# Second block of a two-block transformer kernel: ten gate tiles moved beside the mixers, the merge as a phase of its own, output projection by token halves with the last norm

## The reference, cut to what matters

```python
h = _rms_norm(x, g_pre)
proj = h @ w_in + b_in            # 54 column tiles of 128 for the mixers, then 40 for the gates
# five mixers, each 512 wide: y_a (gated delta rule), y_b (31-tap convolution, layer norm),
# y_c (sliding window with sinks), y_d (linear recurrence), y_e (cross attention); y_x = mixer * silu(z_x)
branch_out = jnp.einsum('bsnw,nwd->bsnd', ys, w_br)
gate = jax.nn.sigmoid(gates.reshape(B, S, N_BRANCHES, D_MODEL))
merged = jnp.sum(gate * branch_out, axis=2)
y = merged @ w_out
x = x + _rms_norm(y, g_post)      # mean over the 1024 columns of one token
```

## Time and profile before

| | us |
|---|---|
| median of 3 runs | 3455.55 (3450.47 to 3455.75) |
| the profiled execution's own time | 3458.23 |
| its span in the trace | 3456.4 |
| TensorE busy in the span | 3206.3 (93%) |
| first to last `gemm` unit of the second block, and the rest up to the end | 1602.0 to 3411.2, 45.2 |

### The profile page before, as it was taken

One profiled execution on the slowest core, in us unless ns is written; L12 is line 12 of the kernel. 1 busy time (PEld: TensorE's weight loads), 2 busy tenths in 40 slices (PEclk: granted clock), 3 DMA queues, 4 the chain that ended last, 5 costly groups with the idle time before them and its releaser, 6 DMA issues. The chain is left out here.

```text
span 3456.4 us, 36380 instructions
## 1 busy us (share of the span) xinstructions
PE 3206.3 (93%) x14817; PEld 2466.1 (71%) x14817; DVE 1443.4 (42%) x1849; ACT 1097.4 (32%) x1632; POOL 669.2 (19%) x317
## 2 busy tenths in 40 slices
PE   6999988879999999995999999999999999999995
PEld 4765544447788888874767787777777888888874
DVE  3113333536414141475456877668552213223123
ACT  4334433323312030342453322223434323223122
POOL 2222111014222222242121000011111222222220
PEclk9999999889999999997999999999999999999997
DMA  3211000013111111123332121104334221221121
GB/s 125 97 63 60 19 0 1 1 64 108 49 49 46 48 48 49 49 89 137 100 108 92 37 68 44 61 34 141 110 110 164 92 98 49 98 98 49 49 92 55
DMA packets 105933, 246.19 MB, mean 71 GB/s; under 512 B 8232, under 2 KB 49448, under 8 KB 105640
## 3 DMA queue, kind: packets, MB, share of 16 engines
q1 hardware_dynamic: 97992, 215.56, 19.3%
q10 hardware_dynamic: 7776, 28.32, 2.0%
HBM read 187.74 MB, written 55.05 MB: 70 GB/s over the span
## 5 line engine op out<-in xcount | busy, mean ns | idle before, releaser
L1676 PE MATMUL psum<-normed_hi,w_hi 128*128 128x512 f32 x1632 | 674.3, 413 | 42.4 <-POOL w_lo L2218 35.2
L1678 PE MATMUL psum<-normed_hi,w_lo 128*128 128x512 f32 x1632 | 639.4, 392 | 0.0
L1677 PE MATMUL psum<-normed_lo,w_hi 128*128 128x512 f32 x1632 | 638.2, 391 | 0.0
L2218 POOL TENSOR_TENSOR w_lo<-buffer,w_hi 128x1024 fp32r<-128x1024 f32 x122 | 310.0, 2541 | 1500.8 <-ACT w_hi L1250 1500.8
L1676 PEld LDWEIGHTS psum<-normed_hi,w_hi 128*128 128x128 f32 x1632 | 308.8, 189 | 114.9 <-POOL w_lo L2218 36.7
L1678 PEld LDWEIGHTS psum<-normed_hi,w_lo 128*128 128x128 f32 x1632 | 307.6, 188 | 66.1
L1677 PEld LDWEIGHTS psum<-normed_lo,w_hi 128*128 128x128 f32 x1632 | 308.9, 189 | 63.7 <-issue 8.0
L2839 POOL TENSOR_TENSOR w_lo<-buffer,w_hi 128x1024 fp32r<-128x1024 f32 x88 | 212.4, 2415 | 724.9 <-ACT w_hi L2757 724.9
L1250 ACT ACTIVATE buffer<-psum,par 128x512 f32<-128x512 f32 (+1 forms) x196 | 138.0, 705 | 518.6 <-PE psum L1678 503.4
L2719 PE MATMUL psum<-hidden_hi,w_hi 128*128 128x512 f32 x512 | 200.9, 392 | 3.1 <-POOL w_lo L2839 3.1
L2719 PE MATMUL psum<-normed_hi,w_hi 128*128 128x512 f32 x512 | 200.1, 391 | 3.3 <-POOL normed_lo L2846 2.2
(11 more groups left out here) (393 smaller groups left out, 5438.5 us busy)
## 6 DMA issues: line engine op xcount, KB each, us to landing
buffer<-in_w_mlp SPq DMA_DIRECT2D x72, 512.0 KB, 3.6
buffer<-in_w_in SPq DMA_DIRECT2D x70, 512.0 KB, 4.9
scratch_in<-buffer ACTq DMA_DIRECT2D x54, 512.0 KB, 2.9
buffer<-in_w_gate SPq DMA_DIRECT2D x40, 512.0 KB, 3.6
buffer<-scratch_in SPq DMA_DIRECT2D x32, 512.0 KB, 6.5
buffer<-scratch_y SPq DMA_DIRECT2D x20, 512.0 KB, 7.7
buffer<-in_w_br SPq DMA_DIRECT2D x20, 512.0 KB, 3.6
buffer<-in_w_o SPq DMA_DIRECT2D x16, 512.0 KB, 3.7
```

The costliest lines, as they stand in the source:

```text
L1676: pe.matmul(out, hi, xh, start=k == 0, stop=False)
L1677: pe.matmul(out, hi, xl, start=False, stop=False)
L1678: mm = pe.matmul(out, lo, xh, start=False, stop=k == unit.kc - 1)
L2218: pool.tensor_tensor(ws.lo[:, n % 2], raw[:, n % 2], ws.hi[:, n % 2].bitcast(F32), ALU.subtract).then_inc(w_lo, 1)
```

## The change

The second block becomes two phases. (1) `mixer_phase` keeps only the mixers and the input projection, and ten of the forty gate tiles (tiles 6 and 7 of each branch, `EARLY_GATES`) are put among the input tiles: `Stream` has 130 units where the part up to the end of the input projection had 110. The planned end stays at 1040 (`T_END`, once `T_MERGE`), so that units 34 to 86 are planned in the 466 us that held 34 to 74, and 86 to 130 in the 324 us that held 74 to 110. The early gates are evicted with the sigmoid and stored to HBM. (2) `merge_phase` has the other 30 gate tiles, the branches and the output projection, with a ring of six PSUM banks; the stored gates come back by SP for the last two tiles of each branch. (3) The output projection runs all eight tiles for the first 512 tokens and then all eight for the last 512, so each of its weight tiles is loaded and split twice (16 slots where there were 8); each half is squared, summed, scaled, added to the residual (3 of 8 tiles by GpSimd) and stored in 256 KB pieces, the first half beside the second half's matmuls. The last norm phase is gone. In the first block `raw` and `w_hi`, `w_lo` only get their names elsewhere, at the same addresses.

```diff
+EARLY_GATES = [b * DC + t for b in BRANCHES for t in (DC - 2, DC - 1)]
+IN2_ORDER = (list(range(12, 16)) + list(range(12))
+             + ["ab", 16, 17, 28, 29, 54, 18, 19, 24, 25, 55, 26, 27, 20, 21, 56, 30, 31, 32, 57, 33, 22, 23, 58]
+             + [34, 35, 36, 37, 59, 38, 39, 40, 41, 60, 42, 43, 44, 45, 61, 46, 47, 48, 49, 62, 50, 51, 52, 53, 63])
...
-    pace = Pace((0, 0.0), (34, 250.0), (74, T_AFTER), (110, T_MERGE), (st.n_merge, T_MERGE + 654.0),
-                (st.n_merge + 16, T_MERGE + 742.0))
+    pace = Pace((0, 0.0), (34, 250.0), (86, T_AFTER), (len(st.units), T_END))
...
-                            run(halves(res[:, q % 3])[h], ps, ACT.Identity, bias=shift).then_inc(kept_act, 1)
+                            run(halves(res[:, q % 3])[h], ps, ACT.Identity if j < N_IN2 else ACT.Sigmoid, bias=shift).then_inc(kept_act, 1)
...
+            def ends():
+                yield T_END + 60.0
+                for r in range(3):
+                    sp.wait_ge(stored[r], 16 * ((len(held) + 2 - r) // 3))
+                for r in range(2):
+                    sp.wait_ge(wy_out[r], 8 * U)
+                sp.wait_ge(conf_out, 16 * BT)
+                sp.wait_ge(o_out, 16 * NB)
+                sp.wait_ge(lru_out, 16 * BT)
...
+                self.slots.append(("br", tiles[0]))
+                last = b == BRANCHES[-1] and pair == DC // 2 - 1
+                for n, (t, h) in enumerate([(0, 0), (1, 0), (0, 1), (1, 1)] if last else [(0, 0), (0, 1), (1, 0), (1, 1)]):
+                    self.add("br", tiles[t], h, n == 0, BT, t * BT)
+        self.starts.append(self.at)
+        for h in range(2):
+            for j in range(DC):
+                self.slots.append(("out", j))
+                self.add("out", j, h, True, DC, 0)
...
+        def by_pool(j):
+            return j % 2 == 1 and j < DC - 1
...
+                        if unit.kind == "br" and unit.tile % DC == 0 and unit.half == 0:
+                            pe.wait_ge(y_lo, BT * BRANCHES.index(unit.tile // DC) + k + 1)
+                        if unit.kind == "out" and unit.tile == 0:
+                            if k < DC - 2:
+                                pe.wait_ge(merged_lo, k + 1)
+                            else:
+                                pe.wait_ge(half_lo, 2 * unit.half + k - DC + 3)
...
+            def norm():
+                for h in range(2):
+                    yield out_end[h] + 3.0
+                    pe.wait_ge(gathered, (DC - 1) * (h + 1))
+                    if h:
+                        pe.wait_ge(logged, 1)
+                    pe.matmul(n_sum, m.c(C_ONE), total[:, h], start=True, stop=True).then_inc(summed, 1)
...
+                for h in range(2):
+                    for j in range(DC):
+                        yield out_end[h] + 5.4 + (2.0 if h == 0 else 0.7) * j
+                        q = h * DC + j
+                        part = halves(out[:, j])[h]
+                        if j == 0:
+                            dve.wait_ge(rooted, h + 1)
+                        dve.scalar_tensor_tensor(part, part, m.p("post_g", j), total[:, h], ALU.mult, ALU.mult).then_inc(scaled, 1)
+                        if not by_pool(j):
+                            dve.wait_ge(scaled, q + 1)
+                            dve.wait_ge(res_in[q % 4], 16 * (q // 4 + 1))
+                            dve.tensor_tensor(part, part, halves(res[:, j])[h], ALU.add).then_inc(done_dve, 1)
...
 def second_block(nc, m, d):
     mixer_phase(nc, m, d)
-    m.clear(top=A_WORK, end=A_ACT)
-    norm_phase(nc, m, m.act, m.act, m.p("post_g", 0, 8), DC, (m.take(2, S), m.take(S)), residual=m.res, out=d["out"])
+    merge_phase(nc, m, d)
```

More of the change, by code:

```diff
@@ L441, in front_phase, with row_of @@
     T = MLA_H * NB
+    rows_order = list(range(NB))
+    def row_of(t):
+        return rows_order[t // MLA_H]
     small = m.take(3, T)
@@ L469, in wide @@
     def wide(t):
-        return max(0, t + 1 - MLA_H * (HALF // P))
+        return sum(row_of(v) >= HALF // P for v in range(t + 1))
     def pair_ready(i):
@@ new lines, in roots @@
+            def roots():
+                for h in range(2):
+                    yield out_end[h] + 3.6
+                    act.wait_ge(summed, h + 1)
+                    run(total[:, h], n_sum, ACT.Ln, bias=m.c(C_EPS, 1), scale=1.0 / D).then_inc(logged, 1)
+                    act.wait_ge(logged, h + 1)
+                    run(total[:, h], total[:, h], ACT.Exp, scale=-0.5).then_inc(rooted, 1)
+            woven(outputs(), roots(), merged_split(), branches(), gates(), weights())
+        @block.gpsimd
@@ L2534, in products @@
                         continue
-                    yield pace(n + 1) + 0.2
-                    b, t, h = unit.tile // DC, unit.tile % DC, unit.half
+                    yield st.end(n) + 0.2
+                    t, h = unit.tile % DC, unit.half
+                    turn, p = BRANCHES.index(unit.tile // DC), st.count("br", n)
                     gate, to = halves(sg[:, t % 2])[h], halves(merged[:, t])[h]
-                    gated = st.index("gate", unit.tile, h)
-                    if n == st.n_in2 + 4:
-                        for r in range(3):
-                            dve.wait_ge(stored[r], 16 * ((len(held) + 2 - r) // 3))
```

592 lines of the change are left out of this document (323 added, 269 removed).

## The result

The changed kernel takes **3424.53 us** (median of 4 runs, 3422.82 to 3431.33), the kernel before 3453.01 on the same chip (4 runs, 3450.39 to 3455.75). The ratio is 0.9918, with a 95% interval of 0.9901 to 0.9935: 28.5 us faster. I had forecast 60.5 us less and 3395. The sign was right and the time lies inside the range, but the size was less than half of the forecast.

What follows compares the result with a forecast made beforehand. TensorE, busy 93% of the span, was taken as the bound. Terms -38 - 26 + 8 - 4 - 2.5 + 2 = -60.5 us, from the median 3455.55, gave 3395 us; 8-in-10 range 3362 to 3427.

Steps and rivals of the forecast that it cites:

- Part 1: Gates beside the mixers: merge 108.9 us shorter, mixer phase 71 longer with 38 absorbed, so -38 us (0 to -74).
- Nothing absorbed: Rival for the mixer phase: k-steps delay the mixers' chain, phase grows by the full 109 us, 3433; chance 0.20.
- the forecast: Likeliest case: 38 us absorbed in the mixer phase, 5 less to 20 more, 3375 to 3400; chance 0.38.
- Waits filled whole: Rival for the mixer phase: every k-step lands in a wait, all 74 us are absorbed, 3359; chance 0.18.
- The weight-load pipe is the limit: Rival: the mixer phase can't exceed the merge's 82% weight-load share, so 29 us are taken up, 3404; chance 0.18.
- Slower: Rival: denser mixer-phase units wait for ScalarE to evict two PSUM banks; phase grows by 138 us, above 3462; chance 0.04.
- Part 2: Tail after the last unit: only the second half's norm, additions and store remain, 19.0 us for 45.2, so -26 us.
- Part 3: New boundary between mixers and merge: 6.0 us gap and 2.0 of lower clock, +8 us; split y wait gone, -4.
- The old wait for the split y: Merge's first branch: loads issued at the phase's start, 22 us ahead of use, so this wait goes away, -4 us.
- Part 4: Output projection: shorter first-unit wait, some 3 us left, -2.5 us; norm matmul and GpSimd's additions ahead of `w_lo`, +2.

Runs made afterwards that it cites:

- the aimed k-steps: Kernel with late sigmoid, sixth-level and later-stores edits, plus 23 k-steps pulled in front of its 13 longest waits for VectorE or ScalarE: 3399.50 us, ratio 0.9836.
- the sixth level: Changed kernel with the last level of the delta rule's inverse planned 1.8 us later, so more k-steps stand ahead of its last product: 3415.69 us, ratio 0.9894.
- both together: Changed kernel with the sixth-level edit, early gates' sigmoid moved to the merge phase, and first-half output stores planned later: 3409.21 us, ratio 0.9861.
- the kernel without early gates: Changed kernel with all forty gate tiles computed in the merge phase and none beside the mixers: 3440.68 us against 3450.73, ratio 0.9962.
- the late sigmoid: Changed kernel with early gates evicted by Identity and the sigmoid applied in the merge phase after they are read back: 3416.29 us, ratio 0.9898.
- the run with the later stores: Changed kernel with the output stores of the first half of the tokens planned later in SP's list: 3420.62 us, ratio 0.9908.

## Why the prediction was right or wrong

**Part 1 failed, at one sentence:** "I take the idle that shows, 29.5 + 8.2 = 38." The ground I gave for it, that VectorE and ScalarE catch up while TensorE is later, is not enough. I had written the correct objection beside it: "most of the 160 extra k-steps fall where nobody waits, so they push the mixer's chain back by their full length." That is what happened. The phase grew by 97.4 us where I had 71, and only 11.5 us were absorbed. The steps: the sum of the work put in was right (104.3 us of busy time against 108.9). The idle time is there to be filled, as the aimed k-steps show. What I sized wrongly is how much of it an even density of k-steps meets, 16.0 us at the waits of before, and what opens again elsewhere, 11.4 us. Three edits bring the phase down again: 5.8 at the sixth level and 5.8 in the table loads alone, 13.7 with both together, 9.9 more by aiming at the other waits. With these the phase lasts 1132.6 us, where I had forecast 1130. An order in which my forecast of this term is right does exist; it is not the one that the change writes. Not tested: the same edits in the kernel without early gates. It has the waits at this level too (6.7 us), so some of the 23.6 us may be gained with or without the moved gates, and the three amounts are not shown to be the missing 26.4 term by term.

**The table loads were missing from the list of costs.** The prediction costed the evictions as if the function did not matter. The earlier trace rows don't show a load, but ScalarE's groups of before did, ten of them in the stretch. By the rows the 35 more loads of the phase are 45 us of ScalarE, and of the 37.5 that the late sigmoid removed the phase gave back 5.8. The Trainium skill (ScalarE: Activation LUTs, What ACT_TABLE_LOAD costs) counts 1283 ns for a load and 1380 ns of drain beside it, paid at each change to a different table set; an estimate by that page is 93 us for the 35. The trace agrees on the 1283 and shows no drain (the rows at the end of this document).

**The rivals.** "Nothing absorbed" was the nearest: it gave 3433 and named the mechanism, "its waits move along with it", and its span of 3410 to 3448 holds the result. I gave it 0.20 and the forecast 0.38. It is half right: of the 16.0 us filled at the old waits 11.4 opened again at others, but of the k-steps aimed at long waits 14.4 of 15.7 us were absorbed there and 4.7 came back elsewhere. "Waits filled whole" did not happen. "The weight-load pipe is the limit" has the closest size after it, 3404, and in the stretch from 1853 to 2404 weight loads are indeed busy 447.68 of 551.00 us, 81%, just the merge's share. The aimed k-steps decide: with them the same units, 34 to 86, take 536 us in place of 554, and the share is 83%, above that of the merge. So it was not the bound:

```profile
1852.70:2389.00 536.30, 527.09 (x3161) 447.02 (x3160) 374.44 (x496) 168.80 (x241) 63.99 (x25) 1.00 0.21 68
```

"Slower" fell: in the whole phase a unit waited once for an eviction, 1.6 us.

**Part 2, the tail, was right:** 19.5 us measured against 19.0. How it came out differs in one detail. VectorE's and GpSimd's additions there:

```profile
3409.80 0.69 DVE L2675 TENSOR_TENSOR buffer<-buffer,res 128x512 f32<-128x512 f32 x1
3411.23 1.70 POOL L2597 TENSOR_TENSOR buffer<-buffer,res 128x512 f32<-128x512 f32 x1 [16.98 <-DVE buffer L2671]
3411.85 1.63 DVE L2675 TENSOR_TENSOR buffer<-buffer,res 128x512 f32<-128x512 f32 x1
```

An addition of VectorE takes 0.69 us alone and 1.63 when it meets GpSimd's, and it ends 0.55 us behind the end of that one. This happens at all three, 0.94 us each and 2.8 us in sum; I had charged two with 1.2 each, 2.4. The exclusive lock of the Trainium skill (SBUF — State Buffer, SBUF: two separate sides) has the count right, all three, where I had two; the 3.6 us that I had worked out for it is too much, so my sum came out near by two errors that cancel.

**Part 3, the boundary, was right:** 6.5 us from the last unit to the first of the merge, against 6.0, and the first matmuls behind it start 0.43 us apart, the lower of the two clock levels, as I had assumed. This lasts longer than I took: against 0.227 us a matmul, 2.8 us are lost up to 2767.5, where I had 2.0. The old wait for the split y is gone.

**Part 4 was right within its bounds.** The merge without the tail got shorter by 107.3 us where the terms gave 111.4. One wait of 3.7 us for `w_lo`, with the slower matmuls behind it, costs 5.8 us by the run with the later stores, more than the whole 4.1 that are missing. Against it stands the first output unit: the wait of some 3 us for the stored gates that I had left there did not come. I had looked for the wait for `w_lo` in GpSimd's list, behind its additions; it came from SP's list, where stores waited for VectorE's late additions and a weight read stood behind them.

**The sum:** +26.4 in the mixer phase, +4.1 in the merge, +0.5 in the gap and +0.3 in the tail make 31.3 us on top of the forecast. The profiled spans differ by 32.5 us, of which 3.2 lie ahead of the block in work that the change leaves alone; the medians, which I take for the result, by 28.5.

## What to carry to other kernels

Idle time of an in-order engine can be filled only at the places where it waits: list the waits one by one with what stands ahead of each, and count only the new work that lands there; an even spread of 160 k-steps over a phase filled less than a third of the 38 us that were idle. When work moves to another phase, write down which function ScalarE runs for it and which it runs around it there. And when a busy share of 93% suggests one bound, take most of that engine's work out once, and read the granted clock beside the time: if the phase hardly moves at the same clock, a chain between engines binds as well, and the order of the list is worth more than the amount of work. Here the clock fell too, so the aimed k-steps, and not that run, are the proof.

## What the runs showed of the hardware

- A table load costs ScalarE 1.283 us and nothing around it that a record shows. In the changed kernel an activation starts at 1867.86 and lasts 1.06, the load starts at 1868.94 and lasts 1.28, the next activation starts at 1870.23, so 10 ns behind the load's end; 70 of the 92 loads of the trace have the next activation 11 or 12 ns behind them:

```profile
1867.86 1.06 ACT L1129 ACTIVATE buffer<-buffer 128x1024 f32<-128x1024 f32 x1
1868.94 1.28 ACT L1129 ACT_TABLE_LOAD   x1
1870.23 0.69 ACT L1129 ACTIVATE buffer<-psum,par 128x512 f32<-128x512 f32 x1
```

- What a load costs the kernel is not its length, and it differs from place to place: 27 of them (34.6 us) lengthened a phase by 13.5 us, 0.5 us each, and 29 of them in a phase with more for TensorE to do by 5.8 us, 0.2 us each.
- With 264 us of TensorE's busy time taken out of a phase of 1059, 42 us came back, at a granted clock of 0.86 in place of 0.99: TensorE, idle for 270 us of the phase instead of 48, was granted less clock, and the small matmuls that were left took 163 ns each from start to start in place of 123. A test that takes work away measures this too.
